# Routing tokens to experts: slots compared as block and place, ids formed on the slot's partition, first weight splits behind the ids

## The reference

```
logits = (h @ w_router) + b_router
top_v, top_i = lax.top_k(logits, TOP_K)              # TOP_K = 2 of N_EXPERTS = 8
gates = jax.nn.softmax(top_v, axis=-1)
combine = jnp.sum(jax.nn.one_hot(top_i, N_EXPERTS) * gates[..., None], axis=-2)
for e in range(N_EXPERTS):
    out = out + combine[..., e:e + 1] * swiglu(h, w1[e], w3[e], w2[e])
```

## Time and profile before

| | us |
|---|---|
| runs, median of 3 | 2060.86 (2058.14 to 2061.54) |
| the profiled execution | 2056.73 |
| its span, first to last instruction | 2055.1 |
| PE busy in the span | 1768.7 (86%) |
| DVE busy | 1332.1 (65%) |
| ACT busy | 811.4 (39%) |
| POOL busy | 282.4 (14%) |

### The profile page before, as it was taken

The page is one execution under the profiler, slowest core; times in us unless marked ns, Lnnn a source line. Parts: engine busy times, 40 slices in busy tenths (PEclk is TensorE's granted clock), DMA queues, the critical chain, the costliest instruction groups (busy, mean ns, idle before and its releaser), DMA issues.

```text
span 2055.1 us, 32397 instructions
## 1 busy us (share of the span) xinstructions
PE 1768.7 (86%) x11246; PEld 1586.7 (77%) x11247; DVE 1332.1 (65%) x2391; ACT 811.4 (39%) x1300; POOL 282.4 (14%) x280
## 2 busy tenths in 40 slices
PE   4898799999999999996477976698979799996992
PEld 1596399999999999992333764698968788996992
DVE  0587756568878784478884547244757688884445
ACT  1435424322122222322566433233744577752331
POOL 1000100000000000049910001001010122101012
PEclk9999899999999999995599998799989899998996
DMA  8333323446754351520000003236775799965434
GB/s 237 125 123 124 115 70 93 137 128 200 234 164 144 111 157 52 149 72 20 3 1 0 29 20 113 84 108 198 246 227 165 231 323 331 325 208 179 117 103 165
DMA packets 312650, 289.20 MB, mean 141 GB/s; under 512 B 20874, under 2 KB 301674, under 8 KB 312468
## 3 DMA queue, kind: packets, MB, share of 16 engines
q1 hardware_dynamic: 298292, 249.28, 39.2%
q0 software_dynamic: 12272, 34.50, 5.2%
q10 hardware_dynamic: 1904, 3.13, 0.5%
HBM read 263.38 MB, written 23.47 MB: 140 GB/s over the span
## 4 chain that ended last, share of the span: by engine, by line
PE 73%; DVE 11%; issue 7%; ACT 4%; DMA 2%; ACTq 1%; POOL 0%; DVEq 0%; POOLq 0%; SPq 0%
PE ps L1264 18%; PE ps L1265 18%; PE ps L1266 18%; PE ps L1269 6%; PE ps L1270 3%; PE ps L1376 2%; DVE vp L2343 2%; PE ps L1307 1%; DVE lo L1977 1%; PE ps L1326 1%; ACT hi L770 1%; PE ps L1586 1%; DMA raw<-in_moe_w_dram 1%; PE ps L1701 1%; DVE hot L2579 1%
## 5 line engine op out<-in xcount | busy, mean ns | idle before, releaser
L1977 DVE TENSOR_TENSOR lo<-raw,hi 128x1024 fp32r<-128x1024 f32 (+3 forms) x442 | 458.1, 1057 | 246.8 <-ACT hi L770 242.8
L770 ACT ACTIVATE hi<-raw 128x1024 fp32r<-128x1024 f32 (+3 forms) x442 | 394.5, 919 | 563.6 <-PE ps L1266 483.8
L1264 PE MATMUL ps<-h_wide,hi 128*128 128x320 f32 (+1 forms) x1728 | 541.7, 314 | 34.6 <-issue 28.4
L1265 PE MATMUL ps<-h_wide,hi 128*128 128x320 f32 (+1 forms) x1728 | 537.2, 311 | 0.0
L1266 PE MATMUL ps<-h_wide,lo 128*128 128x320 f32 (+1 forms) x1728 | 537.1, 311 | 0.0
L1264 PEld LDWEIGHTS ps<-h_wide,hi 128*128 128x128 f32 x1728 | 327.5, 190 | 37.6 <-issue 35.3
L1265 PEld LDWEIGHTS ps<-h_wide,hi 128*128 128x128 f32 x1728 | 327.2, 189 | 0.4 <-issue 0.2
L1266 PEld LDWEIGHTS ps<-h_wide,lo 128*128 128x128 f32 x1728 | 327.3, 189 | 0.0
L1264 PE MATMUL ps<-g_both,hi 128*128 128x320 f32 x528 | 166.7, 316 | 2.6 <-DVE g_both L2284 2.6
L1265 PE MATMUL ps<-g_both,hi 128*128 128x320 f32 x528 | 163.6, 310 | 0.0
L1266 PE MATMUL ps<-g_both,lo 128*128 128x320 f32 x528 | 163.6, 310 | 0.0
(11 more groups left out here) (381 smaller groups left out, 2816.8 us busy)
## 6 DMA issues: line engine op xcount, KB each, us to landing
raw<-in_moe_w_dram SPq DMA_DIRECT2D x160, 512.0 KB, 5.4
raw<-in_w_mod_dram SPq DMA_DIRECT2D x96, 512.0 KB, 4.5
raw<-in_moe_w_dram SPq DMA_DIRECT2D x96, 384.0 KB, 3.7
raw<-in_ff_w_dram SPq DMA_DIRECT2D x40, 512.0 KB, 4.8
raw<-in_moe_w_dram SPq DMA_DIRECT2D x64, 256.0 KB, 3.5
y_rows<-zeros POOLq DMA_DIRECT2D x22, 512.0 KB, 4.5
raw<-in_ev_w_in_dram SPq DMA_DIRECT2D x12, 512.0 KB, 5.7
raw<-in_ff_w_dram SPq DMA_DIRECT2D x16, 384.0 KB, 4.2
```

The costliest lines, as they stand in the source:

```text
L770: act.activation(hi[c % 2][:, parts[h]], raw[slot][:, parts[h]], ACT.Copy).then_inc(hi_done, 1)
L1264: pe.matmul(out, w_hi, v_hi, start=first, stop=False, skip_group_check=True)
L1265: pe.matmul(out, w_hi, v_lo, start=False, stop=False, skip_group_check=True)
L1977: dve.tensor_tensor(lo[c % 2][:, parts[h]], raw[ring_of(c) % 4][:, parts[h]], hi[c % 2][:, parts[h]].bitcast(F32), ALU.subtract).then_inc( ...
```

## The change

- The splits of MOE and MOE + 1 move on ScalarE behind the copies of `hrows`, on VectorE behind the writing of `ids`.
- Small operations over all five tiles are one instruction with broadcast operands where they were five or ten (`lg`, `members`, the products with the gates, base addresses). `members` is overwritten by the gated products and then compared anew. The token ids are written to `tok_w` before the logits are awaited.
- The ranks take two matmuls of 48 and 40 columns: one with the triangle `BEFORE` over all tiles, one with `ones` over `passed`, the running sum of `both` over tiles, which VectorE makes with a copy and four additions. They come after the fourth group of `hf` and not after the tenth.
- A slot (0 to 639) is split into block (0 to 4) and place (0 to 127). `hot[e]` compares `iota_p` (0 to 127) with the place: five instructions of 128 elements for each expert, in eight buffers of their own. `info` holds for each token, expert and block the four values, zero but in its own block. TensorE takes `hot` as weights (128 columns) and `info` as moving operand (20 columns), five matmuls for each expert; the result has the slot's place on the partition, and goes straight to `ids` and `slot_w`. The copies by ScalarE (L1094) and the transposes (L1692) are gone.
- The tables of counts come after the one-hots. Ids are copied in two groups, experts 0, 2, 4, 6 and then 1, 3, 5, 7. The output slots come last.

The core of the diff (placing of the buffers and the plain folding of small operations left out):

```diff
 # ScalarE
-            for c in range(2):
-                split_hi(MOE + c)
-
             act.wait_ge(r_mm, 1)
 ...
                     act.activation(gw[:, :, 1], gw[:, :, 1], ACT.Exp).then_inc(r_exp, 1)
-
-            for e in range(NE):
-                act.wait_ge(r_info, e + 1)
-                if e:
-                    act.wait_ge(r_info_turned, e)
-                act.activation(info_t[:, :].rearrange("p (h t) -> p h t", h=2), ps[0:4, 4 + 2 * (e % 2):6 + 2 * (e % 2), 0:TH],
-                               ACT.Copy).then_inc(r_info_kept, 1)
+            for c in range(2):
+                split_hi(MOE + c)
 # TensorE
-                if g == 9:
+                if g == 3:
 
                     pe.wait_ge(r_members, 1)
-                    for t in range(TT + 1):
 ...
+                    pe.matmul(ps[:, 5, 0:NE * (TT + 1)], mats[:, BEFORE, :], both[:, :, :].rearrange("p t e -> p (t e)"),
+                              start=True, stop=False, skip_group_check=True)
+                    pe.matmul(ps[:, 5, NE:NE * (TT + 1)], ones[:, :], passed[:, :, :].rearrange("p t e -> p (t e)"),
+                              start=False, stop=True, skip_group_check=True).then_inc(r_ranks, 1)
+
+            for e in range(NE):
+                pe.wait_ge(r_hot, e + 1)
+                for t in range(TT):
+                    last = pe.matmul(ps[:, 6 + e % 2, 4 * TT * e:4 * TT * (e + 1)], hot[e][:, t, :],
+                                     info[:, t, e, :, :].rearrange("p b c -> p (b c)"), start=t == 0, stop=t == TT - 1, skip_group_check=True)
+                last.then_inc(r_info, 1)
 # VectorE
-            for c in range(2):
-                split_lo(MOE + c)
 ...
-            for t in range(TT):
-                for k in range(2):
-                    last = dve.tensor_scalar(members[:, k, t, :], iota8[:, :], ixf[:, t, k:k + 1], None, ALU.is_equal)
+            for k in range(2):
+                last = dve.tensor_tensor(members[:, k, :, :], each_tile(iota8[:, :]), over(ixf[:, :, k:k + 1], NE), ALU.is_equal)
 ...
+            last = dve.tensor_copy(passed[:, 0, :], both[:, 0, :])
+            for t in range(1, TT):
+                link(last)
+                last = dve.tensor_tensor(passed[:, t, :], passed[:, t - 1, :], both[:, t, :], ALU.add)
+            last.then_inc(r_members, 1)
 ...
+            slot_of = comb
+            link(dve.scalar_tensor_tensor(out=slot_of[:, :, :], in0=rank[:, :, :], scalar=1.0, in1=both[:, 0:TT, :], op0=ALU.add, op1=ALU.mult))
+            link(dve.tensor_scalar(slot_of[:, :, :], slot_of[:, :, :], -1.0, None, ALU.add))
+            link(dve.tensor_scalar(block_of[:, :, :], slot_of[:, :, :], float(P), None, ALU.is_ge))
+            for b in range(2, TT):
+                link(dve.scalar_tensor_tensor(out=block_of[:, :, :], in0=slot_of[:, :, :], scalar=float(P * b), in1=block_of[:, :, :],
+                                              op0=ALU.is_ge, op1=ALU.add))
+            link(dve.scalar_tensor_tensor(out=slot_of[:, :, :], in0=block_of[:, :, :], scalar=-float(P), in1=slot_of[:, :, :],
+                                          op0=ALU.mult, op1=ALU.add))
+            for b in range(TT):
+                last = dve.tensor_scalar(own_block[:, :, b], block_of[:, :, :].rearrange("p t e -> p (t e)"), float(b), None, ALU.is_equal)
+            link(last)
+            dve.wait_ge(iota_in, 16)
+            for c in range(4):
+                last = dve.tensor_tensor(info[:, :, :, :, c].rearrange("p t e b -> p (t e) b"), own_block[:, :, :],
+                                         tok_w[:, :, :, c:c + 1].bitcast(F32).rearrange("p t e c -> p (t e) c").to_broadcast([P, NE * TT, TT]), ALU.mult)
+            link(last)
+
+            for e in range(NE):
+                for t in range(TT):
+                    last = dve.tensor_scalar(hot[e][:, t, :], iota_p[:, :], slot_of[:, t, e:e + 1], None, ALU.is_equal)
+                last.then_inc(r_hot, 1)
 # ... the tables of counts, as before, up to r_tables
+            for p in range(2):
+                dve.wait_ge(r_info, NE - 1 + p)
+                v = ps[:, 6 + p, 0:4 * TT * NE].rearrange("p (e g c) -> p e g c", e=NE, c=4)[:, p:NE:2]
+                dve.tensor_copy(ids[:, p:NE:2, :], v[:, :, :, 0])
+                link(dve.tensor_copy(slot_w[:, p:NE:2, :], v[:, :, :, 1]))
+                dve.tensor_tensor(slot_w[:, p:NE:2, :], slot_w[:, p:NE:2, :], v[:, :, :, 2], ALU.add).then_inc(r_ids, NE // 2)
+
+            for c in range(2):
+                split_lo(MOE + c)
 ...
-                for t in range(TT):
-                    last = dve.tensor_scalar(hot[e % 2][:, t, :], iota_t[:, :], rank[:, t, e:e + 1], None, ALU.is_equal)
-                last.then_inc(r_hot, 1)
```

More of the change, by code:

```diff
@@ L250, in hybrid_trunk_step @@
         hrows = place("hrows", [P, TT, D], at=scratch + 4 * KT * T)
[L251 to L254, removed]
+        iota_p = place("iota_p", [P, P], at=scratch + 8 * KT * T)
+        info = place("info", [P, TT, NE, TT, 4], F32R, at=scratch + 8 * KT * T + 4 * P)
+        at_hot = scratch + 8 * KT * T + 4 * P + 16 * TT * NE * TT
+        hot_a = place("hot_a", [P, 4, TT, P], F32R, at=at_hot)
+        hot_b = place("hot_b", [P, 3, TT, P], F32R, at=at_spare)
+        hot_c = place("hot_c", [P, 1, TT, P], F32R, at=at_hh + 8 * KT * HW - 4 * TT * P)
+        hot = [hot_a[:, e] for e in range(4)] + [hot_b[:, e] for e in range(3)] + [hot_c[:, 0]]
+        top = max(top, at_hot + 16 * TT * P)
         scratch_end, here[0] = here[0], at_tmp
@@ L270, in hybrid_trunk_step @@
         lgt = place("lgt", [NE, T])
-        info_t = place("info_t", [4, T])
+        own_block = place("own_block", [P, NE * TT, TT])
         assert here[0] <= at_tmp + 16 * PADW
@@ L412, in hybrid_trunk_step @@
         r_info = sem("r_info")
-        r_info_kept = sem("r_info_kept")
-        r_info_turned = sem("r_info_turned")
         r_ids = sem("r_ids")
@@ L2519, in _ @@
             link(dve.tensor_tensor(gw[:, :, 1], gw[:, :, 1], gw[:, :, 0], ALU.mult))
[L2520 to L2523, removed]
+            for k in range(2):
+                last = dve.tensor_tensor(members[:, k, :, :], members[:, k, :, :], over(gw[:, :, k:k + 1], NE), ALU.mult)
@@ L2524, in _ @@
             link(last)
+            link(dve.tensor_tensor(comb[:, :, :], members[:, 0, :, :], members[:, 1, :, :], ALU.add))
             link(dve.tensor_copy(tok_w[:, :, :, 1], comb[:, :, :]))
             dve.tensor_tensor(tok_w[:, :, :, 2], comb[:, :, :], tok_w[:, :, :, 1].bitcast(F32), ALU.subtract)
-            for t in range(TT):
-                for c in (0, 3):
-                    last = dve.tensor_scalar(tok_w[:, t, :, c], iota8[:, :], 0.0, tok_id[:, t:t + 1], ALU.mult, ALU.add)
+            for k in range(2):
+                last = dve.tensor_tensor(members[:, k, :, :], each_tile(iota8[:, :]), over(ixf[:, :, k:k + 1], NE), ALU.is_equal)
@@ L2551, in _ @@
             dve.tensor_copy(tiles_before[:, :], cnt[0:1, 0, :]).then_inc(r_tables, 1)
-            link(dve.tensor_copy(rank[:, :, :], ps[:, 5, 0:NE * TT].rearrange("p (t e) -> p t e", t=TT)))
-            for t in range(TT):
-                last = dve.tensor_tensor(lg[:, t, :], rank[:, t, :], base8[:, :], ALU.add)
-            link(last)
+            for p in range(2):
[4 more added lines that the diff above has]
+                dve.tensor_tensor(slot_w[:, p:NE:2, :], slot_w[:, p:NE:2, :], v[:, :, :, 2], ALU.add).then_inc(r_ids, NE // 2)
```

68 lines of the change are left out of this document (18 added, 50 removed).

## The result

The changed kernel is slower: 2091.62 us (median of 5 runs, 2087.56 to 2095.04) beside 2060.49 (2058.14 to 2061.54) for the kernel before, ratio 1.0148 [1.0128, 1.0168] (the brackets are a 95% interval). Forecast were 2048.4. The profiled execution has a span of 2090.0 us, 34.9 more than the 2055.1 of before.

What follows compares the result with a forecast made beforehand. Between router logits and first expert matmul, ScalarE's splits, VectorE's one-hots and TensorE's wait for all ids were taken as the bound; ids 20.9 us earlier, less 8.4 waiting for rows, left 12.45: 2048.4 us, range 2041 to 2055.

Steps and rivals of the forecast that it cites:

- Logits copied: Router: ScalarE's copy can start at 1236.23 and takes 0.70; VectorE reads the turned logits at 1237.55, 2.26 us earlier.
- One-hots begin: Router on VectorE: one-hot comparisons start at 1248.5 instead of 1256.10, after small operations summing to 5.96 us.
- operations tensor by tensor: VectorE before the one-hots: four products of 200 elements, 1.3 us together; strided and broadcast operands could add 0 to 2.
- The 40 comparisons: VectorE's one-hots, now 128 elements each instead of 640: 0.205 us each, 8.25 in all, ending at 1256.75.
- Second gather issued: GpSimd gathering the first expert's rows: second gather at 1264.9, landing about 1271.8 while sharing DMA with 2.1 MB of weights.
- Rival (c): Weights go ahead of the gathers, second gather near 1275.5; with slow strided operations the gain is 6.7, 2054 us; 12%.
- the sum: Whole kernel: ids 20.9 us earlier, 8.4 lost waiting for rows, 12.45 left; predicted 2048.4 us.
- Turn: TensorE's first turn of the gathered rows: at 1271.9, 12.45 us before the former 1284.35.
- The 22.6 us after it stay, the experts too: From the turn of the rows to the first expert matmul 22.6 us, unchanged, and the experts' time unchanged as well.
- rival (b): Stalls at expert boundaries grow because code moves: 15.6 plus at least 8.37 for one more boundary, 24.0, so 2072.4; 4%.
- parts 2 to 4: Small router operations, block-and-place one-hots, ids to rows: one-hots 5.3 us earlier beyond the logits' 2.26, ids 20.9 earlier overall.
- part 1: First weight splits moved behind the ids on VectorE, behind the row copies on ScalarE: logits read 2.26 us earlier.

Runs made afterwards that it cites:

- pad_both: Changed kernel plus start-up waits, 15 instructions on ScalarE and 17 on VectorE, putting their expert loops where the kernel before had them: 2046.31 us, ratio 0.9929.
- pe_back: pad_both plus 245 instructions at the start of TensorE's program, putting its loop too where the kernel before had it: 2053.25 us, ratio 0.9972.
- splits_first: pad_both with the splits of the first two expert weights put back ahead of the logits on both engines: 2046.21 us, ratio 0.9916.

## Why the prediction was wrong

By its steps, from the end of the router's input (1235.13 before, 1236.64 after, 1236.95 in pad_both):

- Logits copied 1.1 us after it, as forecast; VectorE reads them 2.4 us after (forecast 2.42).
- Exponential done 6.6 us after (forecast 7.4).
- One-hots begin 12.8 us after (forecast 13.4). The operations tensor by tensor took 1.63 us (forecast 1.3); strided and broadcast operands cost no more than these 0.3 us.
- The 40 comparisons took 7.93 us, a step of 0.20 (forecast 0.205, 8.25). The end of the kernel has the same form in 3.32 us, as in the earlier trace rows.
- The ids of the first four experts are complete 24.3 us after, at 1260.93 (forecast 25.3): 1.0 us early by now.
- Second gather issued 29.35 us after (forecast 29.8), landing 37.05 (forecast 36.7). More than half of that was lost on GpSimd, whose copy took 1.24 us and not the 0.37 of the earlier trace rows; the landing took 7.70 us (forecast 6.9), within the 8.1 of the earlier trace rows, beside 2.10 MB of weights. Rival (c) is in this stage, but already in the sum.
- Turn 37.4 after, forecast 36.8; from the turn to the first expert 21.4 us, forecast 22.6. The gain at the first expert is 71.82 - 58.86 = 13.0 us, in pad_both 12.7, forecast 12.45.
- In pad_both the rest takes 747.5 us from the first expert matmul to the end, before 748.2; from the turn to the end 769.8, within 3 of the 770.8 forecast. Its ratio, 0.9929 [0.9904, 0.9955], is 14.6 us [9, 20], which holds the 12.45. But pad_both moves TensorE's loop too. With that loop back in its place (pe_back) the whole gain is 5.8 us [3.5, 7.8]. So the sum is borne out up to the first expert, and its last step, that this gain reaches the end of the kernel whole, only with TensorE's loop where the change put it; that it did there is in part luck.

**The step that failed** is "The 22.6 us after it stay, the experts too", and with it the size and chance of rival (b). The 22.6 us became 21.4; the experts and what follows took 794.5 us and not 748.2. The mechanism stood there: stalls where the program enters another expert's body, and all code behind the edit lying elsewhere. But its price was worked out from the stalls that the trace already had, as if only these could grow, with "one more boundary at least 8.37". The four of them in the earlier trace rows fell by 4.0 us in all. The loss came at the three boundaries that had 2.87, 2.23 and 0.55, where no code was loaded before; these lost 10.3, 10.4 and 12.8 us. Two of them don't even enter another body: they pass through the same one again. A fourth part, 5.96 us, came at a boundary that had a stall, where ScalarE and VectorE had gone on behind it and now didn't. With the three priced at the 8.37 us that the prediction itself gave to one more boundary, the price would have been 25 us beside the clock, twice the gain, and a shift of the loop by 15 and 17 instructions, which I could have counted in the diff, gives no reason to call that a matter of 4%: of the six heads tried on each engine three were bad on ScalarE and two on VectorE.

I cited the Trainium skill ("Runtime: NRT & Kernel Launch", Instruction fetch mechanics) for the rule that a taken branch out of the window that is held forces a fetch before the engine goes on. The runs bear the mechanism out: packets and stalls come and go together. The same section of the Trainium skill says that the instructions come in blocks of 16 KiB (256 instructions) and that two are held. Here a packet on queue 14 is 8 KB, and in pad_both, by the count of its program (no trace shows these numbers), both engines pass through a body of 186 and 178 instructions, to the loop's end 889 and 1051 instructions from its head and back; from 1655 to 1800, over all three boundaries, no packet came on queue 14. The measurement decides: the jump over that distance does not by itself force a load. What does, beside the place, stays open.

What the edit's parts are worth, then: parts 2 to 4 some 12.7 us at the first expert, of which 5.8 to 15 are left at the end, by where TensorE's loop stands; part 1 nothing; the shift of the loop on ScalarE and VectorE +45 us.

## What to carry to other kernels

An edit ahead of a loop that passes through much code changes the loop's place, and that can cost more than the edit gains (45 us against 13 here). Compare the instruction packets of the page's part 3 before and after; if they differ, shift the loop by a few dozen empty instructions on the engines concerned, on all of them at once, before judging the edit. When stalls are priced as a risk, price the boundaries that have none as well.

## What the runs showed of the hardware

- Between two experts of the same code TensorE stood still for 12.0 to 13.2 us where ScalarE and VectorE both loaded code again (8 packets of 8 KB from 1660 to 1682 in the kernel after), and for 2.0 to 3.1 us where they didn't.
- Two engines that load code at the same time stall hardly longer than one (13.2 us and 12.1 with one, 13.2 with both).
- GpSimd's copy of 128x5 numbers took 0.19 us beside VectorE's operations of 128x10 to 128x40 (splits_first) and 1.26 beside its splits of 128x1024 (pad_both); the DMA issue behind it came 1.08 us later.
- Two gathers of 0.5 MB took 4.8 us in the median alone (splits_first) and 7.6 beside 2.1 MB of weight loads (the kernel after).
